# The last additions of a mixture-of-experts layer: two of the four full row tiles given to GpSimd

## The chip, the cores and the metric

The kernel runs on one core of a Trainium2 chip. The core's engines are called here as in the profile: PE (TensorE, matrix products), DVE (VectorE), ACT (ScalarE), POOL (GpSimd) and SP (SyncE, which here only issues DMAs). Each engine works through its own list of instructions and waits on semaphores for the others. The metric is the device time of one execution in microseconds (us). Three runs of the kernel before took 1344.6, 1348.84 and 1351.97 us; the median is 1348.84 us.

## The reference, cut to what matters

One step of a decoder layer for 512 prompt rows and 8 sample rows, 520 rows of 1024 float32 in all. The part that the change touches is the last line of the layer:

```python
x = x + gt1 * merged                       # x1: the residual after attention
h2 = _rmsnorm(x, g_norm_ffn) * (1.0 + sc2) + sh2
x = x + gt2 * _moe(h2, ...)                # MoE: 64 routed experts (8 per row) and one shared expert
# inside _moe:  return (routed + shared).reshape(shp)
```

`gt2` is one row of 1024 gates for the prompt and one for each sample row. The kernel adds `gt2 * shared` early; the routed part is a sum over experts that is gathered in DRAM, and `gt2` times that sum is added to `x1` at the end.

## The kernel before, in words

The 520 rows are held in SBUF as five tiles: four full ones of 128 rows by 1024 columns (`x[:, t, :]`, t = 0 to 3) and one of the 8 sample rows (t = 4). `rows_of` holds their heights. In the profile `x` is called X.

The mixture of experts runs as a list of units (one expert with up to 128 places, or two with 64 each). For each unit POOL gathers the rows of `h2` with an indirect DMA (L1488), PE makes the products, ACT and DVE copy them out, and POOL adds the unit's result to a sum in DRAM with another indirect DMA (L1492, a scatter that adds). There are two such sums, `rsum[0]` and `rsum[1]` (routed_sum in the profile). The second one gets nothing from the last four experts, so it is loaded and added while PE still works; the first one is complete only when the last unit's scatter has landed.

`add_sum(t, n)` (L1159 to L1165, on DVE) takes tile t of sum n, which SP has loaded into `rows[t][n]` (reg_q in the profile), multiplies it in place by the gates (L1163), waits for that product, and adds it to X (L1165). Each of the two raises `y_step` by one. The gates are `row(3, t, 0, D)`: `RB` in reg_s for the full tiles, where the gate row stands in all 128 partitions, and `RS` for the sample rows (cst in the profile). The tiles of sum 1 are added in the loop over the last units; the tiles of sum 0 come at the very end, in the order 0 to 4, and are the last work of DVE.

The end of the program is this chain. POOL waits at L1532 and L1533 until every scatter has landed, and raises `routed_done`. SP waits for that and for the ten steps of sum 1 (L1465 and L1466), and issues five loads of sum 0 (L1469), one for each tile: 512 KB for a full tile, 32 KB for the sample rows. DVE runs `add_sum(t, 0)` as the loads land (semaphores load_in0 to load_in4). For each tile SP waits for its addition (L1472) and issues the store of the tile to the output y (L1473), in the order 0 to 4. At last SP waits for all stores. PE and ACT have nothing to do in this stretch.

POOL has used only memsets and DMAs up to here: a memset of 128x1024 (L1660), one of 128x2048 (L1484), and the DMAs that it issues. `zero_set` is the semaphore of the first of these memsets; it stands at 1 from then on.

Of the kernel before, what the change touches and what calls it, by code (L numbers as in the profile page):

```python
# [18 lines left out]
D = 1024  # L19
KC = D // P  # L20
SEQ = 512
QB = SEQ // P
NS = 8
T = SEQ + NS
TT = QB + 1
# [143 lines left out]
def into(n):  # L169

    return n % 2 if n < NE - LATE else 0


def added(a, n):

    return sum(into(m) == a for m in range(n))
# [74 lines left out]
def program(nc, I, O):  # L251
    es = ExitStack()
    with es:
# [3 lines left out]
        def sem(name):  # L257
            return es.enter_context(nc.semaphore(name))
# [19 lines left out]
        def view(t, at, shape, parts=P):  # L278
            n = int(np.prod(shape))
            v = t[0:parts, at:at + n]  # L280
            names = "abcd"[:len(shape)]
            if len(shape) > 1:
                v = v.rearrange(f"p ({' '.join(names)}) -> p {' '.join(names)}",
                                **{k: s for k, s in zip(names, shape)})
            return v
# [7 lines left out]
        x = view(X, 0, [TT, D])  # L293
# [137 lines left out]
        zero_set, scattered = sem("zero_set"), [sem(f"scattered{n}") for n in range(2)]  # L431
# [35 lines left out]
        rows_in, ROWS_IN = group_in, [16 * (USES[n] + (n < 3) + 2) for n in range(5)]  # L467
# [9 lines left out]
        y_step = sem("y_step")  # L477
# [6 lines left out]
        rows = [[view(reg_q, 6144 * (1 - n) + t * D, [D]) for n in range(2)] for t in range(TT)]  # L484
# [25 lines left out]
        gidx1 = [g[:, 0:1] for g in gidx]  # L510
        sidx1 = [g[:, 0:1] for g in sidx]
        rows_of = [P] * QB + [NS]
        ROWS = ((0, 2), (1, 4), (2, 3), (3, 5))

        def down_w(b, c):
# [19 lines left out]
        def part(n, places):  # L535

            return slice(HALF * n, HALF * n + HALF) if len(places) == 2 else slice(0, SLOTS)

        def row(v_, t, c0, n):

            return RB[v_][:, c0:c0 + n] if t < QB else RS[v_][:, c0:c0 + n]
# [324 lines left out]
        def vector_after(dve):  # L866
# [291 lines left out]
            def add_sum(t, n):  # L1158

                n_ = rows_of[t]  # L1160
                got, xo = rows[t][n][0:n_, :], x[0:n_, t, :]
                dve.wait_ge(rows_in[t], ROWS_IN[t] - 16 * n)
                V.tensor_tensor(got, got, row(3, t, 0, D), ALU.mult).then_inc(y_step, 1)  # L1163
                dve.wait_ge(y_step, 2 * TT * (1 - n) + 2 * t + 1)
                V.tensor_tensor(xo, xo, got, ALU.add).then_inc(y_step, 1)  # L1165

            for j in range(NU):
                u, a = j % 2, j % AHEAD
                if j + AHEAD < NU:
                    onehot(j + AHEAD)  # L1170
                if j + 1 < NU:
                    gated(j + 1)
                if j + 2 < NU:
                    copy_rows_b(j + 2)
                for n in range(2 if j >= 2 else 0):
                    dve.wait_ge(*landed_sums(n, j - 2))
                V.tensor_copy(sidx1[u], gidx1[a]).then_inc(sidx_set, 1)
                if len(UNITS[j]) == 2:
                    V.tensor_copy(sidx2[u][0:HALF, :], gidx1[a][HALF:SLOTS, :]).then_inc(sidx2_set, 1)
                if j + AHEAD < NU:  # L1180
                    take_ids(j + AHEAD)
                if j == COUNT_AT:
                    steps = r + sum(5 * len(places) - 1 for places in UNITS[:j + AHEAD + 1])
                    dve.wait_ge(route, steps)
                    count_more(steps)
                dve.wait_ge(y_ready, 2 * j + 2)
                V.tensor_copy(y[:, u, 512:1024], pb[7][:, :]).then_inc(yB_set, 1)  # L1187
                if j >= NU - LATE + 1:
                    for t in ((0, 1), (2, 3), (4,))[j - (NU - LATE + 1)]:
                        add_sum(t, 1)  # L1190
# [39 lines left out]
                        V.tensor_copy(y[:, 0, 0:512], pb[6][:, :]).then_inc(yB_set, 1)  # L1230
                        V.tensor_copy(y[:, 0, 512:1024], pb[7][:, :]).then_inc(m_y, 1)

            for t in range(TT):
                add_sum(t, 0)

        def square_x(act, m):
# [128 lines left out]
        def sync_after(sp):  # L1365
# [24 lines left out]
            for n in range(4):  # L1390
                at = (ROWS[n][1] - 2) * D
                sp.dma_start(RS[n][:, :], modd[1:9, at:at + D]).then_inc(mod_rest_in, 16)
# [76 lines left out]
                sp.dma_start(rows[t][0][0:n_, :], rsum[0][t * P:t * P + n_, :]).then_inc(rows_in[t], 16)  # L1469
            for t in range(TT):  # L1470
                n_ = rows_of[t]
                sp.wait_ge(y_step, 2 * TT + 2 * t + 2)  # L1472
                sp.dma_start(O["y"][t * P:t * P + n_, :], x[0:n_, t, :]).then_inc(win_out, 16)  # L1473
            sp.wait_ge(win_out, 16 * (2 * NS + TT))
            sp.wait_ge(big_out, 16 * 10)
# [2 lines left out]
        def pool_after(pool):  # L1478
            pool.wait_ge(aux_free, NAUX)
            pool.dma_start(wr, I["w_router"]).then_inc(wr_in, 16)  # L1480
            pool.wait_ge(h2_out[0], 16 * 3)
            pool.wait_ge(h2_out[1], 16 * 2)
            pool.wait_ge(proj_ready, 2 * TT)
            nc.gpsimd.memset(xg.rearrange("p a b -> p (a b)"), 0.0).then_inc(xg_clear, 1)  # L1484
            pool.wait_ge(xg_clear, 1)

            def gather(u, idx, s):
                nc.gpsimd.indirect_dma_start(xg[:, u, :], None, h2d, bass.IndirectOffsetOnAxis(ap=idx, axis=0),  # L1488
                                             bounds_check=T - 1, oob_is_err=False).then_inc(s, 16)

            def scatter(u, idx, n, of=slice(0, SLOTS)):
                nc.gpsimd.indirect_dma_start(rsum[n], bass.IndirectOffsetOnAxis(ap=idx[0:of.stop - of.start, :], axis=0), y[of, u, :], None,  # L1492
                                             bounds_check=T - 1, oob_is_err=False, compute_op=ALU.add).then_inc(scattered[n], 16)

            def ask(j):
                pool.wait_ge(gidx_set, j + 1)
                if j >= 2:
                    pool.wait_ge(xg_turned, 2 * (j - 2) + 2)
                gather(j % 2, gidx1[j % AHEAD], xg_in[j % 2])

            for j in range(AHEAD):
                ask(j)
            for j in range(NU):
                u = j % 2
                if j + AHEAD < NU:
                    ask(j + AHEAD)
                pool.wait_ge(yA_set, j + 1)
                pool.wait_ge(yB_set, j + 1)
                pool.wait_ge(sidx_set, j + 1)
                for n, p in enumerate(UNITS[j]):  # L1510
                    if n:
                        pool.wait_ge(sidx2_set, sum(len(places) - 1 for places in UNITS[:j + 1]))
                    a = into(LOAD[p])
                    pool.wait_ge(scattered[a], 16 * (ZEROS + added(a, LOAD[p])))
                    scatter(u, sidx2[u] if n else sidx1[u], a, part(n, UNITS[j]))
            pool.wait_ge(route_set, 1)
            more = pool.value_load(over[0:1, 0:1], min_val=0, max_val=OVER)
            with pool.If(more > 0):
                pool.wait_ge(m_over, 1)
                pool.wait_ge(xg_in[0], 16 * (NU // 2))  # L1520
                pool.wait_ge(xg_in[1], 16 * (NU // 2))
                with pool.Fori(0, more) as i:
                    with pool.Fori(0, NE) as e:
                        j = i * NE + e
                        pool.wait_ge(gidx_set, j + (NU + 1))
                        pool.sem_inc(asked, 1)
                        gather(0, gidx1[0], xg_in[0])
                        pool.wait_ge(scattered[0], j * 16 + 16 * (ZEROS + added(0, NE)))
                        pool.wait_ge(m_y, i * (NE + 1) + (e + 3))
                        pool.sem_inc(asked, 1)  # L1530
                        scatter(0, gidx1[0], 0)
            pool.wait_ge(scattered[0], more * (16 * NE) + 16 * (ZEROS + added(0, NE)))  # L1532
            pool.wait_ge(scattered[1], 16 * (ZEROS + added(1, NE)))  # L1533
            pool.sem_inc(routed_done, 1)

        def load_mod_row(sp, n, there):

            at = (ROWS[n][1] - 2) * D
            sp.dma_start(row(n, 0, 0, D), modd[0, at:at + D].unsqueeze(0).broadcast_to([P, D])).then_inc(there, 16)
# [73 lines left out]
        def _(sp):  # L1613
# [33 lines left out]
            for n in range(3):  # L1647
                load_mod_row(sp, n, mod_rows_in)
            sync_after(sp)

        @block.gpsimd
# [289 lines left out]
        def _(dve):  # L1941
# [238 lines left out]
            for k in range(ITERS):  # L2180
# [14 lines left out]
                if k == STEPS + 2:  # L2195
                    scale_x(dve, 1)
            vector_after(dve)

        @block.scalar
# [216 lines left out]
```

## Time and profile before

| | before |
|---|---|
| median of three runs | 1348.84 us (1344.6 to 1351.97) |
| the profiled execution's own time | 1346.66 us |
| its span, from the first to the last instruction | 1344.9 us |
| PE busy | 1182.7 us, 88% |
| DVE busy | 484.6 us, 36% |
| POOL busy | 239.5 us, 18% |

The profile page gives each engine's busy time over the whole span. It has a view of the chain that ended last: from the last instruction it goes back at each step to what released it. Waits are named by the engine that waited and by what ended the wait. DMA rows give the time of the issue, and of loads the time from issue to landing. "DMA" in the view by stretches is the mean busy share of the core's 16 DMA engines.

### The profile page before, as it was taken

To read this page: it belongs to the slowest core of one execution; us is meant where nothing else is said; L and a number is where in the kernel's file an instruction comes from. 1 tells how busy PE (TensorE), PEld (TensorE's weight loads), DVE (VectorE), ACT (ScalarE), POOL (GpSimd) and SP (SyncE) were. 2 spreads that over 40 slices of the span, in tenths; PEclk is the share of its full clock that TensorE was granted. 3 is DMA by queue.
4 is the path that set the end of the run, shared out by engine and by line. 5 is a ranking of instruction groups with operands and counts; after the bars stand their busy time and mean duration, and the time that the engine had idled before them with its cause. 6 is when DMAs were issued, how large, how long until landed. Compare 5 with 4: busy or idle time off the path is not lost.

```text
span 1344.9 us, 17672 instructions
## 1 busy us (share of the span) xinstructions
PE 1182.7 (88%) x5832; PEld 610.4 (45%) x5832; DVE 484.6 (36%) x1388; ACT 273.8 (20%) x612; POOL 239.5 (18%) x281
## 2 busy tenths in 40 slices
PE   4999999957687878999899999998989898989891
PEld 1687774324343335445344444443444443444440
DVE  2356556034453442255623232322232222232226
ACT  2222342023232234021111111111111111111110
POOL 0200000023323220000012222222221121221110
PEclk9999999968888897999999999999999998999996
DMA  9979999999999997999699999999998998998854
GB/s 371 422 286 338 332 370 325 335 284 365 379 347 366 361 393 293 359 318 356 223 353 326 363 385 392 383 383 364 365 383 341 369 344 326 390 373 337 300 170 143
DMA packets 90942, 457.71 MB, mean 340 GB/s; under 512 B 15560, under 2 KB 17128, under 8 KB 73056
## 3 DMA queue, kind: packets, MB, share of 16 engines
q1 hardware_dynamic: 56960, 347.80, 67.3%
q0 software_dynamic: 28384, 80.43, 18.9%
q10 hardware_dynamic: 5504, 28.32, 6.7%
q8 instruction: 48, 0.79, 0.2%
q14 instruction: 46, 0.38, 0.1%
HBM read 435.13 MB, written 106.77 MB: 403 GB/s over the span
## 4 chain that ended last, share of the span: by engine, by line
PE 66%; DMA 17%; DVE 7%; issue 4%; SPq 4%; ACT 1%; ACTq 1%; POOLq 0%; DVEq 0%
PE banks L742 20%; PE banks L766 11%; DMA reg_w<-in_w_down 8%; PE banks L1732 7%; PE banks L575 4%; PE banks L1722 3%; DMA reg_q<-in_w_down 2%; PE banks L729 2%; PE banks L637 2%; DVE reg_s L1988 2%; SPq L1566 2%; PE banks L1857 2%; PE banks L1899 2%; SPq L1567 1%; DMA reg_q<-in_cache_k 1%
## 5 line engine op out<-in xcount | busy, mean ns | idle before, releaser
L742 PE MATMUL banks<-reg_q,reg_w 128*128 128x512 f32 (+1 forms) x624 | 243.8, 623 | 16.1 <-issue 13.6
L742 PEld LDWEIGHTS banks<-reg_q,reg_w 128*128 128x128 f32 (+1 forms) x624 | 93.4, 173 | 143.2 <-issue 143.2
L766 PE MATMUL banks<-reg_q,reg_w 128*128 128x512 f32 (+1 forms) x360 | 142.3, 608 | 3.1 <-DMA reg_w<-in_w_down 2.0
L1144 DVE SCALAR_TENSOR_TENSOR reg_w<-banks,small,reg_w 128x256 f32<-128x256 f32 x50 | 24.2, 484 | 310.5 <-ACT reg_w L1337 310.5
L1492 POOL DMA_INDIRECT routed_sum<-reg_w,sidx x64 | 97.2, 1518 | 160.4 <-issue 85.5
L1488 POOL DMA_INDIRECT reg_w<-h_rows,gidx x50 | 52.3, 1046 | 396.3 <-DVE gidx L1105 388.7
L1337 ACT ACTIVATE reg_w<-banks 128x256 f32<-128x256 f32 x50 | 19.2, 384 | 439.2 <-PE banks L742 439.2
L742 PE MATMUL banks<-reg_s,reg_w 128*128 128x512 f32 (+1 forms) x192 | 89.6, 622 | 7.4 <-issue 7.4
L742 PE MATMUL banks<-hT,reg_w 128*128 128x512 f32 (+1 forms) x208 | 91.9, 595 | 1.3 <-issue 1.3
L1732 PE MATMUL banks<-hT,reg_q 128*128 128x260 f32 x384 | 88.3, 389 | 3.9 <-DVE mod L1954 2.3
L1187 DVE COPY reg_w<-banks 128x512 f32<-128x512 f32 x50 | 34.6, 691 | 131.6 <-PE banks L766 131.6
L1732 PEld LDWEIGHTS banks<-hT,reg_q 128*128 128x128 f32 x384 | 73.6, 193 | 15.7 <-issue 4.3
L1988 DVE RECIPROCAL reg_s<-reg_s 128x520 f32<-128x520 f32 x16 | 54.4, 3398 | 63.3 <-ACT reg_s L2240 63.1
L766 PE MATMUL banks<-reg_w 128*128 128x512 f32 (+1 forms) x152 | 69.6, 636 | 6.1 <-DMA reg_w<-in_w_down 5.6
L766 PEld LDWEIGHTS banks<-reg_q,reg_w 128*128 128x128 f32 (+1 forms) x360 | 49.1, 167 | 53.5 <-issue 52.2
L1722 PE MATMUL banks<-reg_w,hT 128*128 128x512 f32 x128 | 56.0, 594 | 1.5 <-ACT reg_q L2254 0.8
L742 PEld LDWEIGHTS banks<-hT,reg_w 128*128 128x128 f32 (+1 forms) x208 | 34.6, 169 | 46.9 <-issue 46.9
L575 PE MATMUL banks<-reg_w,hT 128*128 128x512 f32 x128 | 55.6, 594 | 0.0
L742 PEld LDWEIGHTS banks<-reg_s,reg_w 128*128 128x128 f32 (+1 forms) x192 | 31.7, 169 | 48.5 <-issue 48.5
L1093 DVE TENSOR_SCALAR reg_q<-cst,reg_w 128x128 bf16<-128x128 bf16 (+3 forms) x320 | 53.4, 237 | 0.0
L1353 ACT COPY reg_w<-banks 128x512 f32<-128x512 f32 x50 | 29.3, 585 | 114.4 <-PE banks L766 110.5
L729 PE MATMUL banks<-cst,reg_w 128*128 128x128 f32 x400 | 51.9, 273 | 0.0
(371 smaller groups left out, 1482.8 us busy)
## 6 DMA issues: line engine op xcount, KB each, us to landing
reg_q<-in_w_gate_up SPq DMA_DIRECT2D x39, 2048.0 KB, 33.5
reg_q<-in_w_down SPq DMA_DIRECT2D x39, 1024.0 KB, 34.3
out_win_k_s<-in_win_k SPq DMA_DIRECT2D x8, 4094.0 KB
hT<-in_w_gate_up SPq DMA_DIRECT2D x13, 2048.0 KB, 33.7
reg_s<-in_w_gate_up SPq DMA_DIRECT2D x12, 2048.0 KB, 32.2
out_win_v_s<-in_win_v ACTq DMA_DIRECT2D x6, 4094.0 KB
reg_w<-in_w_ada SPq DMA_DIRECT2D x11, 2048.0 KB, 15.3
reg_w<-in_w_down SPq DMA_DIRECT2D x13, 1024.0 KB, 33.2
```

Of the source, the lines that this page charges most:

```text
L575: last = mm(pb[n % 4][0:n_, :], lhsT=hT[:, k, t * P:t * P + n_], rhs=wslot[h][:, k, :], start=(i == 0), stop=(i == KC - 1))
L729: last = turn(pb[2 + hh][:, c * P:c * P + P], xg[:, j % 2, (hh * 4 + c) * P:(hh * 4 + c + 1) * P], ident)
L742: last = mm(pb[j % 2][of, :], lhsT=xT[:, j % 2, k, of], rhs=wgu[LOAD[p] % NBUF][:, k, :], start=(k == 0), stop=(k == KC - 1))
L766: last = mm(pb[6 + hh][of, :], lhsT=aT[:, j % 2, c, of], rhs=down_w(LOAD[p] % NBUF, c)[:, hh * 512:hh * 512 + 512], start=(c == 0), stop=( ...
L1093: last = V.tensor_scalar(oh[0:n_, t, wide * n:wide * n + wide], slotno[0:n_, 0:wide], slot[0:n_, t, p:p + 1], None, ALU.is_equal)
L1187: V.tensor_copy(y[:, u, 512:1024], pb[7][:, :]).then_inc(yB_set, 1)
L1353: C(y[:, u, 0:512], pb[6][:, :]).then_inc(yA_set, 1)
L1488: nc.gpsimd.indirect_dma_start(xg[:, u, :], None, h2d, bass.IndirectOffsetOnAxis(ap=idx, axis=0), bounds_check=T - 1, oob_is_err=False).th ...
L1492: nc.gpsimd.indirect_dma_start(rsum[n], bass.IndirectOffsetOnAxis(ap=idx[0:of.stop - of.start, :], axis=0), y[of, u, :], None, bounds_chec ...
L1722: last = mm(to[:, 0:512], lhsT=hT[:, k, t * P:t * P + P], rhs=w[:, k, :], start=(k == 0), stop=(k == KC - 1))
L1732: last = mm(to[:, at], lhsT=w[:, k, n % 4 * P:n % 4 * P + P], rhs=moved, start=(k == 0), stop=(k == KC - 1))
L1988: V.reciprocal(rr[:, n % 2, :], rr[:, n % 2, :]).then_inc(rr_set, 1)
```

## The change

Of the last five additions (sum 0), DVE keeps tiles 0 and 2 and the sample rows, in that order. Tiles 1 and 3 go to POOL, as a product and a sum each, with the same operands, in place as before. They stand at the end of POOL's program, behind `routed_done`. POOL waits first for the ten steps of sum 1, then for the load of its tile; its steps raise `zero_set` from 1 to 2, 3, 4 and 5. SP's stores keep their order 0 to 4; those of tiles 1 and 3 wait for POOL's steps instead of DVE's. The steps of `y_step` are renumbered to match.

```diff
+        DVE_LAST, POOL_LAST = (0, 2, QB), (1, 3)
...
                 V.tensor_tensor(got, got, row(3, t, 0, D), ALU.mult).then_inc(y_step, 1)
-                dve.wait_ge(y_step, 2 * TT * (1 - n) + 2 * t + 1)
+                dve.wait_ge(y_step, 2 * t + 1 if n else 2 * TT + 2 * DVE_LAST.index(t) + 1)
                 V.tensor_tensor(xo, xo, got, ALU.add).then_inc(y_step, 1)
...
-            for t in range(TT):
+            for t in DVE_LAST:
                 add_sum(t, 0)
...
             for t in range(TT):
                 n_ = rows_of[t]
-                sp.wait_ge(y_step, 2 * TT + 2 * t + 2)
+                if t in DVE_LAST:
+                    sp.wait_ge(y_step, 2 * TT + 2 * DVE_LAST.index(t) + 2)
+                else:
+                    sp.wait_ge(zero_set, 2 * POOL_LAST.index(t) + 3)
                 sp.dma_start(O["y"][t * P:t * P + n_, :], x[0:n_, t, :]).then_inc(win_out, 16)
...
             pool.sem_inc(routed_done, 1)
+            pool.wait_ge(y_step, 2 * TT)
+            for i, t in enumerate(POOL_LAST):
+                got, xo = rows[t][0], x[:, t, :]
+                pool.wait_ge(rows_in[t], ROWS_IN[t])
+                nc.gpsimd.tensor_tensor(got, got, row(3, t, 0, D), ALU.mult).then_inc(zero_set, 1)
+                pool.wait_ge(zero_set, 2 * i + 2)
+                nc.gpsimd.tensor_tensor(xo, xo, got, ALU.add).then_inc(zero_set, 1)
```

The end of DVE's program before: five products and five sums, tile by tile (load_in0 to load_in4 are the semaphores of the five loads).

```order
L1163 TENSOR_TENSOR reg_q<-reg_q,reg_s 128x1024 [waits load_in0]
L1165 TENSOR_TENSOR X<-X,reg_q 128x1024 [waits y_step]
L1163 TENSOR_TENSOR reg_q<-reg_q,reg_s 128x1024 [waits load_in1]
L1165 TENSOR_TENSOR X<-X,reg_q 128x1024 [waits y_step]
L1163 TENSOR_TENSOR reg_q<-reg_q,reg_s 128x1024 [waits load_in2]
L1165 TENSOR_TENSOR X<-X,reg_q 128x1024 [waits y_step]
L1163 TENSOR_TENSOR reg_q<-reg_q,reg_s 128x1024 [waits load_in3]
L1165 TENSOR_TENSOR X<-X,reg_q 128x1024 [waits y_step]
L1163 TENSOR_TENSOR reg_q<-reg_q,cst 8x1024 [waits load_in4]
L1165 TENSOR_TENSOR X<-X,reg_q 8x1024 [waits y_step]
```

The same place on DVE with the change (the line numbers are one higher):

```order
L1164 TENSOR_TENSOR reg_q<-reg_q,reg_s 128x1024 [waits load_in0]
L1166 TENSOR_TENSOR X<-X,reg_q 128x1024 [waits y_step]
L1164 TENSOR_TENSOR reg_q<-reg_q,reg_s 128x1024 [waits load_in2]
L1166 TENSOR_TENSOR X<-X,reg_q 128x1024 [waits y_step]
L1164 TENSOR_TENSOR reg_q<-reg_q,cst 8x1024 [waits load_in4]
L1166 TENSOR_TENSOR X<-X,reg_q 8x1024 [waits y_step]
```

The four instructions of tiles 1 and 3 are gone from DVE; the six others keep their order.

The end of POOL's program with the change; before, it ended at the ISA row of L1532 (now L1536), behind which nothing but the last two waits stood:

```order
L1522 UNCONDITIONAL_BRANCH
L1536 ISA
L1543 ISA [waits scattered0,scattered1]
L1543 TENSOR_TENSOR reg_q<-reg_q,reg_s 128x1024 [waits load_in1,y_step]
L1545 TENSOR_TENSOR X<-X,reg_q 128x1024 [waits zero_set]
L1543 TENSOR_TENSOR reg_q<-reg_q,reg_s 128x1024 [waits load_in3]
L1545 TENSOR_TENSOR X<-X,reg_q 128x1024 [waits zero_set]
```

POOL now ends with four TENSOR_TENSOR, each pair behind the load of its tile.

SP's stores with the change:

```order
L1470 DMA reg_q<-routed_sum 8x1024
L1477 DMA out_y<-X 128x1024 [waits y_step]
L1477 DMA out_y<-X 128x1024 [waits zero_set]
L1477 DMA out_y<-X 128x1024 [waits y_step]
L1477 DMA out_y<-X 128x1024 [waits zero_set]
L1477 DMA out_y<-X 8x1024 [waits y_step]
```

The stores stand where they stood; the second and the fourth wait for POOL.

## Rows read from the trace of the kernel before

**Rows 1.** Page, first part: busy time, share of the span, instructions.
```profile
PE 1182.7 (88%) x5832; PEld 610.4 (45%) x5832; DVE 484.6 (36%) x1388; ACT 273.8 (20%) x612; POOL 239.5 (18%) x281
```
**Rows 2.** Chain that ended last, from 1320 us on: start us, us, what.
```profile
1320.37 6.29 DMA routed_sum<-reg_w,sidx
...
1326.68 0.05 POOLq L1534
...
1326.82 3.80 DMA reg_q<-routed_sum
...
1330.65 1.24 DVE reg_q L1163
...
1341.47 1.21 DVE X L1165
```
**Rows 3.** Timeline of DVE: start us, us, engine, line, operation, shapes [idle before].
```profile
1330.65 1.22 DVE L1163 TENSOR_TENSOR reg_q<-reg_q,reg_s 128x1024 f32<-128x1024 f32 x1 [10.28 <-DMA reg_q<-routed_sum]
1331.90 1.22 DVE L1165 TENSOR_TENSOR X<-X,reg_q 128x1024 f32<-128x1024 f32 x1
1333.05 1.22 DVE L1163 TENSOR_TENSOR reg_q<-reg_q,reg_s 128x1024 f32<-128x1024 f32 x1
...
1340.23 1.21 DVE L1163 TENSOR_TENSOR reg_q<-reg_q,cst 8x1024 f32<-8x1024 f32 x1
1341.47 1.21 DVE L1165 TENSOR_TENSOR X<-X,reg_q 8x1024 f32<-8x1024 f32 x1
```
**Rows 4.** Timeline of SP, narrow stretches: the fourth and the fifth store.
```profile
1340.34 0.33 SPq L1473 DMA_DIRECT2D out_y<-X  x1
...
1342.71 0.30 SPq L1473 DMA_DIRECT2D out_y<-X  x1
```
**Rows 5.** Stretches at the end: engines' busy us, PEclk, DMA share, GB/s.
```profile
1341.30:1342.60 1.30, 0.00 (x0) 0.00 (x0) 1.26 (x2) 0.00 (x0) 0.00 (x0) 0.50 0.87 356
1342.60:1343.20 0.60, 0.00 (x0) 0.00 (x0) 0.09 (x1) 0.00 (x0) 0.00 (x0) 0.50 0.00 0
1343.20:1343.60 0.40, 0.00 (x0) 0.00 (x0) 0.00 (x0) 0.00 (x0) 0.00 (x0) 0.50 0.47 61
1343.60:1344.90 1.30, 0.00 (x0) 0.00 (x0) 0.00 (x0) 0.00 (x0) 0.00 (x0) 0.50 0.03 6
```
**Rows 6.** Line L1469, 1327.2 to 1327.6 us: the load of tile 1.
```profile
L1469 SPq DMA_DIRECT2D reg_q<-routed_sum x1: 423/423/423, 1327.2 to 1327.2; - x1
...
DMA to landing us min/median/max: 4.7/4.7/4.7
```
**Rows 7.** Line L1469, 1327.9 to 1328.1 us: the load of tile 2.
```profile
L1469 SPq DMA_DIRECT2D reg_q<-routed_sum x1: 432/432/432, 1327.7 to 1327.7; - x1
...
DMA to landing us min/median/max: 6.7/6.7/6.7
```
**Rows 8.** Line L1469, 1328.12 to 1328.3 us: the load of tile 3.
```profile
L1469 SPq DMA_DIRECT2D reg_q<-routed_sum x1: 432/432/432, 1328.2 to 1328.2; - x1
...
DMA to landing us min/median/max: 7.5/7.5/7.5
```
**Rows 9.** Groups of POOL's instructions: line, operation, shape, count | busy, mean ns | idle before.
```profile
L1484 POOL MEMSET reg_w<- 128x2048 f32 x1 | 1.8, 1804 | 94.0 <-DMA h_rows<-reg_s 94.0
...
L1660 POOL MEMSET X<- 128x1024 f32 x1 | 1.0, 951 | 33.5 <-PE banks L1693 33.5
```
**Rows 10.** Page, costliest groups: DVE's longest instruction.
```profile
L1988 DVE RECIPROCAL reg_s<-reg_s 128x520 f32<-128x520 f32 x16 | 54.4, 3398 | 63.3 <-ACT reg_s L2240 63.1
```
**Rows 11.** Timeline of DVE and POOL, 1302 to 1315 us: scatters beside additions.
```profile
1302.35 1.57 POOL L1492 DMA_INDIRECT routed_sum<-reg_w,sidx  x1 [10.11 <-DMA routed_sum<-reg_w,sidx]
...
1302.42 1.23 DVE L1165 TENSOR_TENSOR X<-X,reg_q 128x1024 f32<-128x1024 f32 x1
...
1312.48 1.22 DVE L1163 TENSOR_TENSOR reg_q<-reg_q,reg_s 128x1024 f32<-128x1024 f32 x1
...
1313.37 1.76 POOL L1492 DMA_INDIRECT routed_sum<-reg_w,sidx  x1 [9.45 <-DVE reg_w L1187]
...
1313.72 1.22 DVE L1165 TENSOR_TENSOR X<-X,reg_q 128x1024 f32<-128x1024 f32 x1
```
**Rows 12.** Line L1492: all 64 scatters, ns min/median/max.
```profile
L1492 POOL DMA_INDIRECT routed_sum<-reg_w,sidx x64: 1424/1572/1763, 691.4 to 1320.4; - x64
```

## The prediction

> **What bounds the kernel now.** I read the page's busy shares first, then the chain that ended last, then the timeline of each engine in the last 25 us. Over the whole span PE is the bound, with 88% [rows 1], but the change lies behind PE's last work, so the shares say nothing on it. The chain does [rows 2]: the last scatter lands 6.29 us after its start, POOL passes on that it is done, SP's first load of sum 0 takes 3.80 us, and from 1330.65 us to the end DVE alone carries the chain. The timeline of DVE shows that stretch as ten instructions without a gap that matters [rows 3]: product and sum of one full tile take 2.40 us from start to start (1330.65 to 1333.05), the pair of the sample rows 2.45 us (1340.23 to 1341.47 plus 1.21), although it has 8 partitions instead of 128. DVE ends at 1342.68, SP issues the last store at 1342.71 [rows 4], and the span ends at 1344.9, which is 2.2 us later. So a gain is possible only between 1330.65 and 1342.68, 12.0 us in all.
>
> The store of a full tile ends later than that of the sample rows. The fourth one is issued at 1340.34 [rows 4]; its packets run until about 1342.6, and the small one's until about 1343.6, behind which 1.3 us pass to the end [rows 5]. A full tile stored last therefore takes 2.26 + 1.3 = 3.5 us from its issue to the end of the span, against 2.2 us for the sample rows. This matters, since POOL's second tile may now be the last.
>
> **The part on DVE.** Four instructions leave: two pairs at 2.40 us, 4.8 us in all. Six stay, 2 x 2.40 + 2.45 = 7.25 us. Their loads don't come evenly: tile 1 lands at 1327.2 + 4.7 = 1331.9, tile 2 at 1327.7 + 6.7 = 1334.4, tile 3 at 1328.2 + 7.5 = 1335.7 [rows 6 to 8]; that of the sample rows has no landing in the trace, and I take 1335.7 for it too. DVE alone would then do tile 0 until 1333.05, wait for tile 2, and end at 1334.4 + 2.40 + 2.45 = 1339.25: of the 4.8 us 3.4 are left, since a wait of 1.35 us for the load takes the place of tile 1.
>
> **The part on POOL.** Four instructions of 128x1024 arrive. The trace has no TENSOR_TENSOR on POOL, so I bound it by its memsets: 951 ns for 1024 columns and 1804 ns for 2048 [rows 9], which is 853 ns for 1024 columns that are written and 98 ns besides. The lower end is 0.95 us, as if the two reads came free beside the write. Two streams one after the other would be 98 + 2 x 853 = 1804 ns, three would be 98 + 3 x 853 = 2657 ns. The far upper end is the longest elementwise instruction of the trace, DVE's RECIPROCAL with 3.40 us [rows 10]. I take the middle between two and three streams, 2.23 us, an estimate from these two rows, since the instruction has two streams in and one out. The Trainium skill gives a measured price in "GPSIMD Engine Reference", section 3.1, of 4497 ns for a float32 tensor_tensor of 2048 columns; half of it is 2.25 us, an estimate from that page, by which the sums below change by less than 0.1 us.
>
> The waits add little: a product's semaphore costs 0.03 us before the sum starts, as on DVE (1330.65 + 1.22 to 1331.90) [rows 3]. POOL's wait for the ten steps of sum 1 is long over when the first load lands, and nothing stands behind POOL's new instructions but its last waits. On SP the stores keep their order: a late tile 1 holds back tile 2, and a late tile 3 holds back the sample rows, by 0.33 us for its issue [rows 4].
>
> **Side by side or in turns.** The open term is what the two engines do to each other, as both read two tiles in SBUF, and X, reg_q and reg_s are open to both. The bounds are: nothing (they run side by side), and all of it (only one of the two moves at a time). The nearest rows are scatters that POOL issues while DVE multiplies and adds. The one at 1302.35 took 1.57 us, as always; the one that began at 1313.37 in the middle of a product took 1.76 us [rows 11], the longest of 64 with a median of 1.57 [rows 12]. DVE's instructions beside them took 1.22 or 1.23 us as elsewhere. So the trace shows at most a small hindrance of POOL, but no row shows POOL reading tiles. The choice is between ends that are 4.8 us apart; I take turns, as the one lengthened row lies where the two engines meet, and because four POOL instructions with eight input streams use whatever path is common far more than a scatter's list of rows does.
>
> The Trainium skill has a rule on this, in "SBUF — State Buffer", section "Who interferes with whom": a VectorE instruction with two inputs in SBUF and a GpSimd instruction that reads SBUF shut each other out, and whichever starts first keeps the other waiting until it is done. The rows agree with it only in so far as the scatters, which are DMAs, are hardly touched; the case of the rule itself no run here shows yet. By the rule the sum is that of the forecast, without it that of the first rival.
>
> **The sum.** In turns, from 1330.65: DVE 7.25 us and POOL 4 x 2.23 = 8.92 us make 16.17 us, and seven changes of turn at 0.03 us add 0.2 us. The order is tile 0's product and sum, tile 1's product, tile 2's product, tile 1's sum, tile 2's sum, tile 3's product, the sample rows' product, tile 3's sum, the sample rows' sum; all loads have landed before their turn. The last ends at 1347.0, plus 2.2 us to the end: 1349.2. Tile 3's sum ends 1.2 us earlier, 1345.8, plus 3.5 us: 1349.3. The span of 1344.9 grows by 4.4 us. The profiled execution took 1346.66 us for a span of 1344.9, so it would take 1351.1 us. That execution was 2.2 us faster than the median of the three runs, 1348.84, on which the sum is 1353.2. I forecast the middle of the two, 1352 us: slower by 0.33%. With 1.81 us per POOL instruction it is +2.7 us instead of +4.4, with 2.66 us +6.1.
>
> **Rivals.** First, side by side at full speed. POOL starts tile 1 at 1331.95 and has 4 x 2.23 + 3 x 0.03 = 9.0 us, with tile 3 already landed when it needs it; it ends at 1341.0, and the span 3.5 us later, at 1344.5: 0.4 us less than before, 1347.3 us on the middle of the two times, 1347.75. Even here the gain is small, because POOL's last store is a full tile. With 1.81 us per instruction POOL waits for tile 3 until 1335.7 and ends at 1339.3: 2.1 us less. With 0.95 us DVE would be last, at 1339.25 plus 2.2: 3.4 us less, 1344.3 us; that is the best that the change can do. For it speaks that DVE's time was the same beside the scatters; against it that POOL's was not, once.
>
> Second, in turns and with a dear POOL instruction, which ends clearly slower. The place is POOL's four TENSOR_TENSOR; each 0.1 us above 2.23 us adds 0.4 us to the chain, since nothing covers it. From 2.8 us on the loss passes 6.7 us, 0.5% of the time; at 3.40 us it is 4.4 + 4 x 1.17 = 9.1 us, 1357 us. For it speaks that no such instruction ran on POOL in this trace, so that its first use could carry a cost that no row shows; against it that POOL's memsets run at one rate for both sizes [rows 9].
>
> Third, taking turns in pieces shorter than an instruction, so that only part of the overlap is lost: anything between the forecast and the first rival, at the middle +2 us, 1350 us.
>
> That the change doesn't do what it says I can leave out: the four instructions stand on POOL behind the right loads, and SP's stores wait for them.
>
> **How the numbers follow.** Turns as forecast 0.45, side by side 0.28, in pieces 0.12, turns with a dear instruction 0.15. About 0.5%, 6.7 us, is what a measurement of this kernel can tell from no change; the three runs alone lie 7.4 us apart. Faster by more than that is beyond the best case of -3.4 us, and takes the spread of the runs besides: 0.03. Slower by more: two thirds of the dear case, and the part of the forecast case where the instruction costs near 2.66 us and the runs add the rest, about 0.17 of it: 0.18 together. The rest, 0.79, is within it. The range reaches from the first rival with cheaper instructions, 1347.75 - 2.1 = 1345.6, to the dear case near its upper end on the median's base, 1357.5. The forecast's own range, with 1.81 to 2.66 us, is 1350.4 to 1353.9.
>
> **What would show it.** In the timeline of the changed kernel, turns would show as DVE or POOL instructions that last longer than alone, with spans that fill each other's gaps: DVE's six would take well over 1.22 us each, or POOL's would. Side by side would show DVE's six at 1.2 us, with the wait for tile 2's load. The price of POOL's instruction is its start-to-start time where DVE is idle, after DVE's last. The last store is that of the sample rows if turns hold, issued near 1347; the store of tile 3 is issued near 1341 if they don't. The prediction is wrong if POOL's instruction costs under 1.8 or over 2.7 us, or if DVE's durations don't change.

## The result

| | before | after |
|---|---|---|
| median of the timed runs | 1347.7 us (6 runs, 1342.73 to 1351.97) | 1357.32 us (6 runs, 1355.67 to 1359.92) |
| the profiled execution's own time | 1346.66 us | 1359.92 us |
| its span | 1344.9 us | 1358.2 us |

The changed kernel is slower: the ratio is 1.0071, with a 95% interval of 1.0048 to 1.0093. In a second comparison (the experiment called again below) the medians were 1354.56 us over 9 runs and 1347.52 us over 14, ratio 1.0056 with an interval of 1.0031 to 1.0082. The forecast was 1352 us, slower by 0.33%.

Over the whole program the page shows little. POOL gains 13 us of busy time, and DVE, which lost four instructions of 1.22 us, gains 2.8 us [rows 1]:

```profile
PE 1191.4 (88%) x5832; PEld 616.9 (45%) x5832; DVE 487.4 (36%) x1384; ACT 273.7 (20%) x612; POOL 252.7 (19%) x285
```

The tail shows what happened. This is the timeline of all engines from the loads of sum 0 on (start us, us, engine, line, operation; the row of SP at 1339.77 merges all five stores):

```profile
1333.55 2.42 SPq L1470 DMA_DIRECT2D reg_q<-routed_sum  x5
1337.26 1.23 DVE L1164 TENSOR_TENSOR reg_q<-reg_q,reg_s 128x1024 f32<-128x1024 f32 x1 [10.00 <-DMA reg_q<-routed_sum]
1338.52 1.23 DVE L1166 TENSOR_TENSOR X<-X,reg_q 128x1024 f32<-128x1024 f32 x1
1338.65 3.29 POOL L1543 TENSOR_TENSOR reg_q<-reg_q,reg_s 128x1024 f32<-128x1024 f32 x1 [9.78 <-DMA reg_q<-routed_sum]
1339.77 13.41 SPq L1477 DMA_DIRECT2D out_y<-X  x5
1340.96 2.06 DVE L1164 TENSOR_TENSOR reg_q<-reg_q,reg_s 128x1024 f32<-128x1024 f32 x1 [1.22 <-DMA reg_q<-routed_sum]
1342.03 3.19 POOL L1545 TENSOR_TENSOR X<-X,reg_q 128x1024 f32<-128x1024 f32 x1
1343.06 3.25 DVE L1166 TENSOR_TENSOR X<-X,reg_q 128x1024 f32<-128x1024 f32 x1
1345.18 3.31 POOL L1543 TENSOR_TENSOR reg_q<-reg_q,reg_s 128x1024 f32<-128x1024 f32 x1
1346.23 3.35 DVE L1164 TENSOR_TENSOR reg_q<-reg_q,cst 8x1024 f32<-8x1024 f32 x1
1348.58 3.20 POOL L1545 TENSOR_TENSOR X<-X,reg_q 128x1024 f32<-128x1024 f32 x1
1349.61 3.25 DVE L1166 TENSOR_TENSOR X<-X,reg_q 8x1024 f32<-8x1024 f32 x1
```

At first sight the two engines run side by side, both slowly, with bars of over 3 us. Add start and duration, and the ends tell another story. POOL's four end at 1341.94, 1345.22, 1348.49 and 1351.78, and each time a DVE instruction ends 1.08 or 1.09 us later: 1343.02, 1346.31, 1349.58, 1352.86. From each of these DVE ends to POOL's next end it is 2.18 to 2.20 us; from the end of DVE's second instruction, 1339.75, to POOL's first, it is 2.19 us. So the bars of 3.2 us are 2.2 us of POOL and 1.1 us of DVE in turns, and a bar holds the other engine's turn as well as its own. DVE's pair for the 8 sample rows pays the same turns as that of a full tile. Before, DVE's instructions took 1.22 us throughout [rows 3].

The second part of the loss is not in that list. DVE's last sum ends at 1352.86, and the span at 1358.2: 5.34 us later, where it was 2.2 us before. The instructions at line 253, the end of the program, show why (engine's queue, operation, count: duration in ns, first and last start). After:

```profile
L253 POOLq EVENT_SEMAPHORE  x2: 17/17/17, 1358.0 to 1358.1; - x2
L253 POOLq DRAIN  x1: 9456/9456/9456, 1348.5 to 1348.5; - x1
...
L253 SPq DRAIN  x1: 13/13/13, 1355.1 to 1355.1; - x1
L253 SPq EVENT_SEMAPHORE  x1: 17/17/17, 1358.2 to 1358.2; - x1
```

Before, in the same view:

```profile
L253 POOLq EVENT_SEMAPHORE  x2: 17/17/17, 1344.7 to 1344.8; - x2
L253 POOLq DRAIN  x1: 6197/6197/6197, 1326.8 to 1326.8; - x1
...
L253 SPq DRAIN  x1: 13/13/13, 1344.7 to 1344.7; - x1
```

POOL closes its program with a DRAIN. Before, it ran from 1326.8 to 1333.0, right behind POOL's last work and beside DVE's additions, where it cost nothing. After, POOL's last sum ends at 1351.78, and the DRAIN at 1348.5 + 9.46 = 1358.0, which is 6.2 us behind that sum. SP had all its stores home by 1355.1 and waited for POOL. The view of SP's waits puts this on the wrong engine:

```profile
SPq L1477 <- POOL X L1545: 10.2, 2, 5.1
SPq L1477 <- DVE X L1166: 5.3, 3, 3.8
SPq L253 <- PEq L253: 3.1, 1, 3.1
SPq L253 <- DMA out_y<-X: 1.6, 1, 1.6
```

PE is named for the 3.1 us, but PE had done nothing for over 30 us; all engines meet at the end, and the one that came last was POOL.

I call tail the time from the landing of tile 0's load to the end of the span. It grew from 14.25 us (1330.65 to 1344.9) to 20.9 us (1337.26 to 1358.2), 6.7 us: 3.6 us because DVE ends 15.60 us into it instead of 12.03, and 3.1 us because of the DRAIN. That is 0.50% of the time. The rest of the difference between the two profiled spans, 6.6 us, lies ahead of the tail, where the two programs do the same work.

### The profile page after: what moved, and what is told of

Same layout as the page of the kernel before. It is cut to its first block, busy times and chain, and to the rows that moved or that the text cites. A ratio compares the mean times of both kernels' runs of the same rounds, so it can differ in the third digit from the quotient of the medians.

```text
span 1358.2 us, 17675 instructions
## 1 busy us (share of the span) xinstructions
PE 1191.4 (88%) x5832; PEld 616.9 (45%) x5832; DVE 487.4 (36%) x1384; ACT 273.7 (20%) x612; POOL 252.7 (19%) x285
## 4 chain that ended last, share of the span: by engine, by line
PE 61%; DMA 19%; DVE 7%; SPq 5%; issue 4%; ACT 2%; ACTq 1%; POOLq 0%; DVEq 0%
PE banks L743 19%; PE banks L767 11%; DMA reg_w<-in_w_down 10%; PE banks L1743 7%; PE banks L576 4%; PE banks L1733 3%; DMA reg_q<-in_w_down 2%; SPq L1577 2%; SPq L1578 2%; PE banks L730 2%; PE banks L638 2%; DVE reg_s L1999 2%; PE banks L1910 1%; ACTq L2294 1%; PE banks L1868 1%
## 5 line engine op out<-in xcount | busy, mean ns | idle before, releaser
L1492 POOL DMA_INDIRECT reg_w<-h_rows,gidx x50 | 52.3, 1047 | 395.6 <-DVE gidx L1106 387.9
L2313 ACT COPY hT<-banks 128x128 f32<-128x128 f32 (+3 forms) x64 | 24.0, 427 | 143.3 <-PE banks L1843 142.0
```

## The experiments

**The changed kernel again.** No edit.

> The changed kernel once more, against the kernel before. Called the tail here: the time from the landing of tile 0's load (start of the first product, 1330.65 us before, 1337.26 us after) to the end of the span; it was 14.25 us before and 20.9 us after, 6.7 us more. Theory (all of the loss is in the tail; what lies ahead of it differs only by the spread of the runs): tail 20.9 us again, time 6.7 us or 0.50% over the kernel before. Rival (the part ahead of the tail became slower too, since the medians of six runs lie 9.6 us apart): 9.6 us or 0.71% again, and the first load of sum 0 is issued near 1333.5 us again instead of 1326.8.

Measured: 1354.56 us over 9 runs against 1347.52 us over 14, a difference of 7.0 us; the span of the profile was 1353.0 us.

```profile
1328.02 2.69 SPq L1470 DMA_DIRECT2D reg_q<-routed_sum  x5
1332.03 1.23 DVE L1164 TENSOR_TENSOR reg_q<-reg_q,reg_s 128x1024 f32<-128x1024 f32 x1 [10.36 <-DMA reg_q<-routed_sum]
```

The first product starts at 1332.03, so the tail is 21.0 us; POOL's DRAIN ends 6.2 us after its last sum again. The first load of sum 0 is issued at 1328.02, not near 1333.5. So the tail repeats, and the 9.6 us of the first comparison did not. Both intervals contain the 0.50% of the tail. The issue of that load is a good measure of what comes ahead of the tail: in the nine profiles of this study it lies between 1321.1 and 1335.5 us, and the latest of all is from late_wait below, whose program up to there is that of the kernel before. No pattern goes with the change. One goes with the clock granted to PE, a mean over the span as a share of full speed: it is 0.944 to 0.947 in the four profiles where this load is issued before 1327 us, and 0.933 to 0.939 in the five where it is issued at 1328 us or later. The six runs of the changed kernel in the first comparison had 0.937 in the mean; in the repeat both kernels had 0.941. What sets the clock no run here shows.

**POOL alone, then DVE.**

```diff
+            dve.wait_ge(zero_set, 5)
             for t in DVE_LAST:
                 add_sum(t, 0)
```

> DVE starts its three tiles only when POOL has done both of its own. Theory (one engine moves at a time, POOL's instruction alone costs 2.2 us): POOL's four take 2.2 us each instead of the 3.2 to 3.3 of the profile after, DVE's six 1.22 us; POOL ends 1.3 + 8.9 = 10.2 us into the tail, DVE 7.25 us later, tail 17.5 + 2.2 = 19.7 us. Rival (POOL's instruction costs 3.25 us by itself and the two only slow each other a little): POOL's four still take 3.2 to 3.3 us, tail 1.3 + 13.0 + 7.25 + 2.2 = 23.8 us.

Timeline of POOL and DVE, then POOL's DRAIN:

```profile
1338.00 2.33 POOL L1544 TENSOR_TENSOR reg_q<-reg_q,reg_s 128x1024 f32<-128x1024 f32 x1 [9.88 <-DMA reg_q<-routed_sum]
1340.42 2.33 POOL L1546 TENSOR_TENSOR X<-X,reg_q 128x1024 f32<-128x1024 f32 x1
...
1345.12 2.34 POOL L1546 TENSOR_TENSOR X<-X,reg_q 128x1024 f32<-128x1024 f32 x1
1347.49 1.23 DVE L1164 TENSOR_TENSOR reg_q<-reg_q,reg_s 128x1024 f32<-128x1024 f32 x1 [21.28 <-POOL X L1546]
...
1353.53 1.21 DVE L1166 TENSOR_TENSOR X<-X,reg_q 8x1024 f32<-8x1024 f32 x1
```
```profile
L253 POOLq DRAIN  x1: 8596/8596/8596, 1345.1 to 1345.1; - x1
```

Alone, POOL's instruction takes 2.33 us and DVE's 1.22. The rival, 3.25 us of its own, is out. The time was 1359.07 us in one run. DVE's first product does not mark the landing of tile 0 here, since DVE starts late; the load is issued at 1332.85 and lands 3.7 us later, so the tail is 1357.4 - 1336.55 = 20.85 us, about 1.1 more than expected: POOL needs 9.46 us instead of 8.9, and the five stores now come within 5 us and end a little later. Doing one engine's work wholly after the other's thus costs no more (20.85 us) than letting them run together (20.9), but not because the additions end as early: DVE's last sum ends 18.2 us into the tail, 2.6 us later than in the changed kernel. POOL's DRAIN, however, ends at 1353.7, before that sum, so that nothing waits for it.

**The kernel before, with a late wait on POOL.** POOL does no arithmetic.

```diff
             pool.sem_inc(routed_done, 1)
+            pool.wait_ge(y_step, 4 * TT)
```

> The kernel before, in which POOL does no arithmetic but waits at the end of its program for DVE's last addition. Theory (at its program's end POOL needs a DRAIN of 6.2 us, which before ran from 1326.8 to 1333.0 beside DVE's work, and after from the end of POOL's last sum at 1351.8 to 1358.0): the DRAIN ends 6.2 us after DVE's last sum, tail 12.05 + 6.2 + 0.2 = 18.4 us instead of 14.25. Rival (the 3.1 us that SP waits at the end after the last store come from POOL's arithmetic or from PE, which the profile names): tail 14.25 us as before.

The first and the last of DVE's ten instructions, and the end of the program (line 253):

```profile
1339.13 1.22 DVE L1163 TENSOR_TENSOR reg_q<-reg_q,reg_s 128x1024 f32<-128x1024 f32 x1 [10.32 <-DMA reg_q<-routed_sum]
...
1349.95 1.21 DVE L1165 TENSOR_TENSOR X<-X,reg_q 8x1024 f32<-8x1024 f32 x1
```
```profile
L253 POOLq DRAIN  x1: 6197/6197/6197, 1351.4 to 1351.4; - x1
L253 SPq COMPARE_BRANCH  x1: 38/38/38, 1353.0 to 1353.0; - x1
L253 SPq DRAIN  x1: 13/13/13, 1353.2 to 1353.2; - x1
L253 SPq EVENT_SEMAPHORE  x1: 17/17/17, 1357.7 to 1357.7; - x1
```

The DRAIN takes 6197 ns, to the nanosecond what it took before, and it starts when the wait is over. The first product starts at 1339.13 and the span ends at 1357.8: tail 18.7 us, expected 18.4. Nothing but one wait was added, and the tail is 4.4 us longer (the one run took 1359.56 us); SP waits 4.6 us behind its stores, which the profile again puts on PE. So the 3.1 us of the changed kernel need no arithmetic on POOL: a bare wait that keeps POOL's program open until late in the tail brings such a loss.

**Tiles 0 and 1 on POOL instead of 1 and 3.**

```diff
-        DVE_LAST, POOL_LAST = (0, 2, QB), (1, 3)
+        DVE_LAST, POOL_LAST = (2, 3, QB), (0, 1)
```

> The changed kernel with tiles 0 and 1 on POOL and tiles 2, 3 and the sample rows on DVE, the same number of instructions on each. Theory (turns, and the DRAIN on the path): POOL starts with the first landing and runs alone until tile 2 lands at 3.75 us, its last sum ends near 11.05 us, its DRAIN near 17.3 us; DVE ends near 15.8 us, tail 15.8 + 2.2 = 18.0 us instead of 20.9. Rival (the 3.1 us at the end come with any arithmetic on POOL, wherever it stands): tail 21.1 us, with SP waiting 3 us after the last store again.

```profile
1335.87 2.33 POOL L1543 TENSOR_TENSOR reg_q<-reg_q,reg_s 128x1024 f32<-128x1024 f32 x1 [8.40 <-DMA reg_q<-routed_sum]
1338.29 2.33 POOL L1545 TENSOR_TENSOR X<-X,reg_q 128x1024 f32<-128x1024 f32 x1
1339.63 2.07 DVE L1164 TENSOR_TENSOR reg_q<-reg_q,reg_s 128x1024 f32<-128x1024 f32 x1 [14.02 <-DMA reg_q<-routed_sum]
1340.58 3.32 POOL L1543 TENSOR_TENSOR reg_q<-reg_q,reg_s 128x1024 f32<-128x1024 f32 x1
```
```profile
L253 POOLq DRAIN  x1: 9459/9459/9459, 1343.9 to 1343.9; - x1
```

The tail is 18.2 us (1335.87 to 1354.1; expected 18.0), 2.7 us less than with tiles 1 and 3, with the same instructions on each engine. POOL starts with the first landing, takes 2.33 us while it is alone and 3.2 to 3.3 when DVE joins, and ends early enough that its DRAIN ends at 1353.4, which is 1.5 us after DVE's last sum but before SP has its last store home at 1353.9. SP's wait at the end is 0.2 us. The single run took 1355.87 us.

**DVE with one operand from SBUF.** ACT copies the gate rows to PSUM before the tail; DVE's products go to PSUM and its sums read them there. POOL has tiles 1 and 3 as in the change.

```diff
...
+                V.tensor_tensor(made, got, two[0 if t < QB else 1][0:n_, :], ALU.mult).then_inc(y_step, 1)
+                dve.wait_ge(y_step, 2 * TT + 2 * i + 1)
+                V.tensor_tensor(xo, xo, made, ALU.add).then_inc(y_step, 1)
...
+            C(two[0][:, :], row(3, 0, 0, D)).then_inc(gates_up, 1)
+            C(two[1][0:NS, :], row(3, QB, 0, D)).then_inc(gates_up, 1)
```

> The changed kernel, tiles 1 and 3 on POOL, but DVE reads at most one operand of each instruction from SBUF: ACT copies the gate rows to PSUM before the tail, DVE's products go to PSUM, and its sums read them there. Theory (what keeps the two apart is DVE's second operand in SBUF): both run side by side, DVE's six at about 1.25 us, POOL's four at 2.33 us as when it was alone; POOL ends 1.3 + 9.45 = 10.75 us into the tail, its DRAIN at 17.0, tail 17.2 us instead of 20.9. Rival (any two arithmetic instructions of DVE and POOL keep each other waiting): 2.2 + 1.1 us turns as in the changed kernel, tail 20.9 us.

Timeline of DVE (banks are PSUM), then of POOL:

```profile
1324.85 1.23 DVE L1166 TENSOR_TENSOR banks<-reg_q,banks 128x1024 f32<-128x1024 f32 x1 [9.98 <-DMA reg_q<-routed_sum]
...
1329.03 1.23 DVE L1166 TENSOR_TENSOR banks<-reg_q,banks 128x1024 f32<-128x1024 f32 x1 [1.69 <-DMA reg_q<-routed_sum]
1330.29 1.22 DVE L1168 TENSOR_TENSOR X<-X,banks 128x1024 f32<-128x1024 f32 x1
1331.43 1.21 DVE L1166 TENSOR_TENSOR banks<-reg_q,banks 8x1024 f32<-8x1024 f32 x1
1332.67 1.21 DVE L1168 TENSOR_TENSOR X<-X,banks 8x1024 f32<-8x1024 f32 x1
```
```profile
1328.61 2.34 POOL L1558 TENSOR_TENSOR X<-X,reg_q 128x1024 f32<-128x1024 f32 x1
1330.91 2.34 POOL L1556 TENSOR_TENSOR reg_q<-reg_q,reg_s 128x1024 f32<-128x1024 f32 x1
1333.32 2.34 POOL L1558 TENSOR_TENSOR X<-X,reg_q 128x1024 f32<-128x1024 f32 x1
```

Both engines now run at the speed they have alone, at the same time. The tail is 17.25 us (1324.85 to 1342.1), as expected; the one run took 1343.88 us. DVE is done 9.0 us into it; the tail is still 3.0 us longer than the 14.25 us of the kernel before, because POOL's own 9.5 us and the DRAIN behind them end last. So it is DVE's second operand in SBUF that brings the turns, and not the tiles that they share: reg_q and X are still used by both. The edit moved two more things, which other rows settle. The products' results went to PSUM too, but the sums still write SBUF and take 1.22 us beside POOL. And DVE no longer reads the gates in reg_s, but the product of the sample rows, which reads its gates from cst, took 3.35 us in the changed kernel all the same. The rule of the Trainium skill that the prediction weighed ("SBUF — State Buffer", section "Who interferes with whom") says this: two inputs in SBUF shut out a GpSimd instruction that reads SBUF, one does not. The runs agree with both halves: 3.2 us bars with two, 1.23 and 2.34 us with one.

**One tile on POOL,** tile 0, first with the operands in SBUF, then with DVE's gates and products in PSUM by the edit above.

```diff
-        DVE_LAST, POOL_LAST = (0, 2, QB), (1, 3)
+        DVE_LAST, POOL_LAST = (1, 2, 3, QB), (0,)
```

> Only tile 0 on POOL, the rest on DVE, operands in SBUF as in the changed kernel. Theory (turns): POOL's product 2.33 us, DVE's product 1.1, POOL's sum 2.2, DVE's sum 1.1, then DVE alone 7.2 us: DVE ends at 13.9 us, POOL's DRAIN lies beside that, tail 16.1 us against 14.25 of the kernel before, a loss of 1.9 us although DVE has two instructions fewer. Rival (side by side, if the turns come only when POOL has several tiles): DVE ends at 11.0 us, tail 13.2 us.

> Only tile 0 on POOL, and DVE with the gates and the products in PSUM. Theory (no turns, DRAIN hidden): POOL ends at 4.7 us and its DRAIN at 10.9; DVE does tile 1 from its landing at 1.3 us, then tiles 2, 3 and the sample rows, and ends at 11.0 us, tail 13.2 us, 1.0 us less than the kernel before: 0.08%, which shows in the tail and not in the time (ratio 0.995 to 1.004). Rival (turns in spite of PSUM): tail 16.1 us.

With SBUF operands the tail was 16.1 us (1330.63 to 1346.7; the one run took 1348.39 us), with PSUM 13.5 us (1328.66 to 1342.2); before it was 14.25. The first four instructions of DVE and the two of POOL, with SBUF operands:

```profile
1331.80 2.25 DVE L1164 TENSOR_TENSOR reg_q<-reg_q,reg_s 128x1024 f32<-128x1024 f32 x1 [11.03 <-DMA reg_q<-routed_sum]
1334.08 3.25 DVE L1166 TENSOR_TENSOR X<-X,reg_q 128x1024 f32<-128x1024 f32 x1
1337.25 1.21 DVE L1164 TENSOR_TENSOR reg_q<-reg_q,reg_s 128x1024 f32<-128x1024 f32 x1
1338.50 1.22 DVE L1166 TENSOR_TENSOR X<-X,reg_q 128x1024 f32<-128x1024 f32 x1
```
```profile
1330.63 2.33 POOL L1543 TENSOR_TENSOR reg_q<-reg_q,reg_s 128x1024 f32<-128x1024 f32 x1 [8.25 <-DMA reg_q<-routed_sum]
1333.05 3.20 POOL L1545 TENSOR_TENSOR X<-X,reg_q 128x1024 f32<-128x1024 f32 x1
```

Even one tile taken off DVE lengthens the tail by 1.8 us, since DVE waits out POOL's turns and saves only 1.2 us for each. With PSUM, DVE's second product:

```profile
1332.73 1.23 DVE L1166 TENSOR_TENSOR banks<-reg_q,banks 128x1024 f32<-128x1024 f32 x1 [0.37 <-issue]
```

The tail is 0.7 us shorter than before, 0.3 less of a gain than expected. DVE stood idle for 0.37 us before the product of tile 2, for which the profile names no cause: the load of that tile, issued at 1325.8, had landed 6.5 us later, at 1332.3. One tile on POOL with DVE's operands in PSUM is the only version with a shorter tail, and it is no faster in the time: 1344.9 us over 12 runs against 1345.22 over 17, ratio 0.9998, interval 0.998 to 1.0016. A gain of 0.05% is far below what the runs can tell.

## Why the prediction was right in direction and short in size

- *The place.* Right. All of the loss that the runs show as the change's own is in the tail, and its length before the change (12.0 us of DVE, 2.2 us behind it) set what could be won.
- *POOL's price.* Right: 2.23 us from the two memsets [rows 9], measured 2.33 us alone and 2.19 us inside a turn. No row decided between the two streams and the three, so that the middle came this close is partly luck.
- *Side by side or in turns.* Turns, as forecast, and the first rival is out. The reason given was thin: a single scatter that was 0.2 us longer [rows 11, 12]. What decided it were the ends in the timeline of the changed kernel and, for the cause, the run with operands in PSUM, not that row.
- *The sum of the turns.* The term was 16.4 us from the first landing to DVE's end; it measured 15.60. In a turn DVE needs only 1.09 us of its 1.22, and a whole turn of both is 3.28 us instead of 2.23 + 1.22 + 0.06; four of them stand behind the 2.49 us of DVE's first pair. The order was as listed.
- *What lies behind the last addition.* This step failed. I took 2.2 us from DVE's last sum to the end, as before [rows 4, 5], and wrote that nothing stands behind POOL's new instructions but its last waits. Behind them stood the DRAIN of 6.2 us; the list of POOL's last instructions ahead of the prediction leaves it out, but the trace of before had it, at a place where it was hidden. It made 5.34 us of the 2.2.
- *The sum.* 4.4 us were forecast and 6.7 measured in the tail: 0.8 us too much for the turns, and 3.1 too little for the end. The medians lay 9.6 and 7.0 us apart. The 1357.32 us of the first comparison lie just inside the range of 1345.6 to 1357.5, whose upper end was set by the dear instruction, which did not come; that the range held is luck.
- *The load of tile 2.* Right: DVE idles 1.22 us for it after tile 0, against 1.35 worked out. It cost the chain nothing, since POOL's first product ran until 1341.94, after that load had landed.
- *The third rival,* turns shorter than an instruction, is out: each DVE instruction ends 1.08 to 1.09 us after a whole instruction of POOL.
- *The second rival,* a dear POOL instruction, is out with 2.33 us; the number it came near (1357 us) had another cause.

That the first measurement came to +9.6 us rather than +6.7 is not settled. It fits the spread ahead of the tail, which the profile of late_wait shows without the change and which goes with the granted clock; and in the repeat, where the mean clock of both kernels was 0.941, the medians lay 7.0 us apart. Of the kernel before, only one of the six runs of the first comparison has its clock on record, 0.944.

## What to carry to other kernels

Moving half of an elementwise stage from VectorE to GpSimd did not split its time here, where both read two tiles from SBUF: the stage took the sum of both, and GpSimd's share cost 1.8 times what it cost on VectorE (2.19 against 1.22 us). If it must be split, put one of VectorE's operands in PSUM, or let GpSimd have its part while VectorE has nothing to do. Even then count GpSimd's own time and its DRAIN: of the six splits measured here only one tile on GpSimd with PSUM operands for VectorE made the tail shorter, by 0.7 us. And read what stands at the end of each engine's program before giving it late work: here GpSimd's closing DRAIN of 6.2 us was free as long as GpSimd was done early.

## What had not been expected of the hardware

GpSimd's DRAIN at the end of the program takes 6197 ns behind a bare wait, in two kernels alike, and ends 6.2 us after the engine's last instruction in all the others. An instruction of VectorE on 8 partitions waits for GpSimd just as one on 128 does. In the profile, instructions that wait for the other engine show as busy: DVE's busy time rose by 2.8 us although it had less to do, so a longer bar at unchanged shape is here a wait.
